# Cross attention scores of the samples: turned keys and TensorE against product-sums on VectorE, with a new order of the sequence buffers

## What is computed

```
xn = rms(h);  p = xn @ w_in
A  = gated DeltaNet (4 heads, chunks of 64; samples: one recurrence step)
B  = latent attention (samples: 2048 cached positions each, in pages)
h += concat(A, B) @ w_out
q  = (rms(h) @ w_xq) as 4 heads of 256
s  = einsum('bthd,bmhd->bhtm', q, mem_k) / 16         # 256 memory tokens
h += einsum('bhtm,bmhd->bthd', softmax(s), mem_v) @ w_xo
h += MoE(rms(h))      # top 4 of 32 experts, w_e1 1024x2048, w_e2 1024x1024 each
y  = rms(h)
```

## Time and profile before

| what | value |
|---|---|
| median of 3 runs | 1478.03 us (1472.29 to 1478.19) |
| the profiled execution: its time | 1474.19 us |
| its span in the trace | 1472.4 us |
| mean granted TensorE clock | 0.977 |
| TensorE busy | 1342.5 us (91%) |
| VectorE busy | 473.3 us (32%) |
| ScalarE busy | 175.9 us (12%) |
| bytes moved | 490.62 MB, mean 333 GB/s |
| `in_w_e` on the chain that ended last | 42% of the span |

### The profile page before, as it was taken

How to read it: one execution, slowest core, us unless ns; L and a number is a source line. 1 busy time by engine, 2 the same in 40 slices (tenths; PEclk the granted TensorE clock), 3 DMA queues, 4 the chain that set the end, 5 groups by cost and what they waited for, 6 DMA issues and landing times.

```text
span 1472.4 us, 19981 instructions
## 1 busy us (share of the span) xinstructions
PE 1342.5 (91%) x8119; PEld 626.1 (43%) x8119; DVE 473.3 (32%) x1082; ACT 175.9 (12%) x343; POOL 48.1 (3%) x45
## 2 busy tenths in 40 slices
PE   8999887999998989999998998998989989889896
PEld 6667543354586453333333233333332333333322
DVE  1856665932033352132222122122221221222213
ACT  1053101221022430000000000000000000000002
POOL 0000211000000420000000000000000000000000
PEclk9999988999999989999999999999999999999999
DMA  9111553636457669999999999999999999999996
GB/s 372 40 36 76 202 209 150 241 112 256 177 223 232 245 254 426 427 426 428 428 428 428 427 428 428 428 428 428 428 428 427 428 428 427 427 427 427 428 427 249
DMA packets 80339, 490.62 MB, mean 333 GB/s; under 512 B 9308, under 2 KB 14528, under 8 KB 28987
## 3 DMA queue, kind: packets, MB, share of 16 engines
q1 hardware_dynamic: 77690, 468.86, 77.2%
q0 software_dynamic: 2304, 20.97, 3.6%
q10 hardware_dynamic: 296, 0.11, 0.0%
HBM read 483.97 MB, written 6.04 MB: 333 GB/s over the span
## 4 chain that ended last, share of the span: by engine, by line
DMA 43%; PE 21%; DVE 2%; ACT 1%; SPq 1%; POOL 1%; issue 1%; DVEq 0%
DMA arena<-in_w_e 42%; PE ps L2032 12%; PE ps L2075 4%; DMA arena<-in_cache_mem_k 1%; PE ps L2103 1%; SPq L1449 1%; PE ps L2117 1%; PE ps L2087 0%; PE ps L2111 0%; POOL arena L2426 0%; POOL arena L2424 0%; DVE arena L2612 0%; DVE arena L2615 0%; DVE arena L2609 0%; PE ps L2062 0%
## 5 line engine op out<-in xcount | busy, mean ns | idle before, releaser
L2032 PE MATMUL ps<-arena 128*64 128x512 f32 x2048 | 460.6, 597 | 54.0 <-DMA arena<-in_w_e 53.0
L2032 PEld LDWEIGHTS ps<-arena 128*64 128x64 f32 x2048 | 146.3, 137 | 346.7 <-issue 293.9
L2075 PE MATMUL ps<-arena 128*64 128x512 f32 x952 | 209.3, 594 | 0.4 <-ACT arena L2289 0.2
L2075 PEld LDWEIGHTS ps<-arena 128*64 128x64 f32 x952 | 67.6, 137 | 136.3 <-issue 128.4
L2609 DVE TENSOR_SCALAR arena<-ps 128x1024 f32<-128x1024 f32 x15 | 18.4, 1225 | 264.7 <-PE ps L2032 264.7
L2627 DVE TENSOR_TENSOR res<-res,ps 128x512 f32<-128x512 f32 x60 | 41.3, 688 | 135.5 <-PE ps L2087 135.5
L2621 DVE COPY arena<-ps 128x512 f32<-128x512 f32 x15 | 10.4, 692 | 209.6 <-PE ps L2075 209.6
L1073 PE MATMUL ps<-arena 32*4 32x512 f32 x640 | 48.9, 657 | 17.5 <-DVE arena L1099 17.5
L1746 PE MATMUL ps<-arena 128*128 128x512 f32 x128 | 55.8, 594 | 0.0
L2018 PE MATMUL ps<-arena 128*128 128x128 bf16 x768 | 54.0, 223 | 1.7 <-DVE arena L2576 1.7
L2087 PE MATMUL ps<-arena 128*128 128x512 f32 x120 | 55.5, 606 | 0.0
(11 more groups left out here) (554 smaller groups left out, 1357.0 us busy)
## 6 DMA issues: line engine op xcount, KB each, us to landing
arena<-in_w_e SPq DMA_DIRECT2D x383, 1024.0 KB, 22.2
arena<-in_w_in SPq DMA_DIRECT2D x8, 1380.0 KB, 17.6
arena<-in_cache_mem_k SPq DMA_DIRECT2D x8, 1024.0 KB, 9.1
arena<-in_w_out SPq DMA_DIRECT2D x2, 2048.0 KB, 8.2
arena<-in_w_xk SPq DMA_DIRECT2D x1, 4096.0 KB, 15.5
arena<-in_w_xv SPq DMA_DIRECT2D x1, 4096.0 KB, 13.6
arena<-in_w_xq SPq DMA_DIRECT2D x1, 4096.0 KB, 23.1
arena<-in_cache_mem_v SPq DMA_DIRECT2D x1, 4096.0 KB, 16.0
```

Source lines behind the costliest of these rows:

```text
L2032: last = pe.matmul(ps[64 * x:64 * x + 64, c, :], xe[:, k, 64 * x:64 * x + 64], weights[x][:, c * 512:(c + 1) * 512], start=False, stop=(k ...
L2075: last = pe.matmul(ps[64 * x:64 * x + 64, 6 + c, :], aT[:, k, 64 * x:64 * x + 64], weights[x][:, j * D + c * 512:j * D + (c + 1) * 512], s ...
```

## The change

Five things are changed.

1. The order of the slots is plain rotation: sequence 6 goes into slot 2 and 7 into slot 3, and GpSimd loads them in the order 4, 5, 6, 7. The half of `w_out` that lies over slot 3 waits for all 8 sequences instead of 7.
2. In the scan's chunk 0, the page step moves behind the state update on VectorE and behind its product on TensorE; the turning of its keys, which was the tail of the last level, moves with it.
3. The mix parts of the prompt's other half for rows 2 and 3 move ahead of the wait for `w_out`'s half 0.
4. `turn_keys`, `KTx` and `qpad` go. 32 small products put the samples' queries into rows of PSUM, ScalarE and VectorE copy them to `q_rows`, two products per sample spread one query row over all 128 partitions in PSUM, and VectorE multiplies raw keys with it and sums (64 `scalar_tensor_tensor` of 128x256 with `accum_out`, one column of `sT` each). 8 products turn `sT` into the bank of the scores. The four `project` of the prompt's `w_xo` part go between the spreads, and VectorE's four joins of the prompt now come ahead of the sample rows', which is the fifth instead of the fourth.
5. ScalarE's order puts the first three bias casts ahead of the exponential. SyncE fills ring slots 1 and 2 ahead of 8 to 11 and 4 to 7, and there are 4 spare buffers instead of 3.

```diff
-    SLOT = (0, 1, 2, 3, 0, 1, 3, 2)
+    SLOT = (0, 1, 2, 3, 0, 1, 2, 3)
...
-        pages_dve(dve, level_step(LEVELS))
+        pages_dve(dve, level_step(LEVELS), False)
...
-        for b in (4, 5, 7, 6):
+        for b in range(NSLOT, DEC):
             pool.wait_ge(sa["pv_done"], max(c for c in range(b) if SLOT[c] == SLOT[b]) + 1)
...
-            for k in chunk_steps(i, 0):
+            for k in chunk_steps(i, 0) if i > 0 else ():
                 pages_dve(dve, k)
...
             last.then_inc(s_ready, 1)
+            if i == 0:
+                turn_keys_of(dve, STEP_SCAN)
+                for k in chunk_steps(i, 0):
+                    pages_dve(dve, k)
...
-            sp.wait_ge(sa["pv_done"], DEC - 1)
+            sp.wait_ge(sa["pv_done"], DEC)
             load_w_out(sp, 0)
...
-            pe.wait_ge(gn["placed"], 1)
+            mix_part(2, range(H, 2 * H))
+            pe.wait_ge(gn["placed"], 2)
+            mix_part(3, range(H, 2 * H))
             pe.wait_ge(wout_gdn_loaded, 16)
...
-    SPARE = 3
+    SPARE = 4
...
+            def spread_query(b):
+                if b >= 2:
+                    pe.wait_ge(sx["scored"], b - 1)
+                for j in range(2):
+                    i = (2 * b + j) % 4
+                    rows = slice(32 * i, 32 * i + DEC)
+                    last = pe.matmul(ps[:, SPREAD_BANKS[b % 2] + j, :], rep1(c_(C_ID, P)[rows, 32 * i + b], [DEC, P]), q_rows[rows, j * 512:(j + 1) * 512],
+                                     start=True, stop=True, tile_position=(32 * i, 0))
+                last.then_inc(sx["spread"], 1)
...
+            for k in range(KD):
+                for i in range(4):
+                    last = pe.matmul(ps[32 * i:32 * i + DEC, 6 + k // 4, (k % 4) * P:(k % 4 + 1) * P], qxT[:, k, SEQ:TOK], ident,
+                                     start=True, stop=True, tile_position=(0, 32 * i))
...
+            def score(b):
+                dve.wait_ge(kx_loaded[b % G], 16 * (b // G + 1))
+                dve.wait_ge(sx["spread"], b + 1)
+                for s in range(2):
+                    if s == 1 and b > 0:
+                        dve.wait_ge(sx["scored"], b)
+                    for h in range(H):
+                        query = ps[:, SPREAD_BANKS[b % 2] + h // 2, (h % 2) * XD:(h % 2 + 1) * XD]
+                        last = nc.vector.scalar_tensor_tensor(products[:, (8 * b + 4 * s + h) % 12], Kx[:, b % G, s, h * XD:(h + 1) * XD], 1.0, query, ALU.mult, ALU.mult,
+                                                              accum_out=sT[:, s, h, b:b + 1])
+                last.then_inc(sx["scored"], 1)
```

More of the change, by code:

```diff
@@ L1303, in scan_pe @@
             last.then_inc(add_made, 1)
+            for k in chunk_steps(i, 0) if i == 0 else ():
+                pages_pe(pe, k)
             for k in chunk_steps(i, 1):
@@ L1465, in build @@
     PARTS = 2 * ((0, 0), (0, 1), (1, 0), (1, 1))
-    cx = {n: sem("cross_" + n) for n in ("keys_stored", "padded", "q_made", "q_moved", "scored", "max", "exp", "probs", "turned", "pt_ready", "out", "out_moved")}
+    cx = {n: sem("cross_" + n) for n in ("keys_stored", "q_made", "q_moved", "scored", "max", "exp", "probs", "turned", "pt_ready", "out", "out_moved")}
     drained = sem("mix_drained")
@@ L1533, in _ @@
             exps(3)
-            act.wait_ge(cx["padded"], 1)
-            for n in range(2 * H):
-                nc.scalar.copy(qpad[:, n].rearrange("p b c -> p (b c)")[:, 0:33 * (DEC - 1) + 1:33], qxT[:, n, SEQ:TOK])
         @block.gpsimd
@@ L1961, in _ @@
             sp.dma_start(pick, const_bf16).then_inc(mo["pick_loaded"], 16)
+            sp.wait_ge(mo["bias_ready"], 1)
+            for n in (1, 2):
+                fill_first(sp, n)
             sp.wait_ge(sx["out"], 1)
@@ L1967, in _ @@
                 fill_first(sp, n)
-            sp.wait_ge(mo["bias_ready"], 1)
-            for n in (1, 2):
-                fill_first(sp, n)
             sp.wait_ge(mo["made"], 5)
-            for i in range(2):
+            for i in range(3):
                 fill(sp, FIRST_SPARE + i, 0, spare[i], spare_full[i])
             sp.wait_ge(mo["logits"], 3)
-            fill(sp, FIRST_SPARE + 2, 0, spare[2], spare_full[2])
+            fill(sp, FIRST_SPARE + 3, 0, spare[3], spare_full[3])
             sp.wait_ge(mo["rounds"], 1)
@@ L2136, in positions @@
                 pe.matmul(ps[0:r, bank, 64:64 + NE], c_(C_BEF, r, r), sel[0:r, t, :], start=not before, stop=True).then_inc(mo["pos"], 1)
-            for m in range(2 * DEC):
-                turn_keys(m)
-                if m >= 2 and m % 2 == 0:
-                    score(m // 2 - 1)
-            score(DEC - 1)
-            pe.wait_ge(wxo_loaded, 16)
-            project(0, 0, 0, range(KD))
+            for k in range(KD):
+                for i in range(4):
+                    last = pe.matmul(ps[32 * i:32 * i + DEC, 6 + k // 4, (k % 4) * P:(k % 4 + 1) * P], qxT[:, k, SEQ:TOK], ident,
+                                     start=True, stop=True, tile_position=(0, 32 * i))
+            last.then_inc(sx["q_turned"], 1)
+            pe.wait_ge(wxo_loaded, 16)
+            project(0, 0, 0, range(0, 3))
+            pe.wait_ge(sx["q_act"], 1)
+            pe.wait_ge(sx["q_dve"], 1)
+            spread_query(0)
+            spread_query(1)
+            project(0, 0, 0, range(3, 6))
+            spread_query(2)
+            project(0, 0, 0, range(6, KD))
+            project(0, 1, 1, range(0, 1))
+            spread_query(3)
+            project(0, 1, 1, range(1, 4))
+            spread_query(4)
+            project(0, 1, 1, range(4, KD))
+            spread_query(5)
+            pe.wait_ge(mo["joined"], 1)
+            project(1, 0, 0, range(0, 4))
+            spread_query(6)
+            project(1, 0, 0, range(4, 7))
+            spread_query(7)
+            project(1, 0, 0, range(7, KD))
+            pe.wait_ge(mo["joined"], 2)
+            project(1, 1, 1, range(0, 4))
+            pe.wait_ge(sx["scored"], DEC)
+            for s in range(2):
+                for h in range(H):
+                    last = pe.matmul(ps[32 * h:32 * h + 32, 4, s * P:(s + 1) * P], sT[:, s, h, :], ident, start=True, stop=True, tile_position=(0, 32 * h))
+            last.then_inc(sx["s_turned"], 1)
+            project(1, 1, 1, range(4, KD))
             pe.wait_ge(sx["probs"], 1)
@@ L2189, in _ @@
             positions(0, 1, ())
-            project(1, 1, 5, range(3, 5))
             turn(1, 0, 2)
@@ L2304, in cast_part @@
                 return nc.scalar.copy(x_part(t, i)[:, a:b], left[t][:, a:b])
-            for m in range(2 * DEC):
-                act.wait_ge(sx["turned"], m + 1)
-                n = m // 2
-                if n >= 2:
-                    act.wait_ge(sx["scored"], n - 1)
-                nc.scalar.copy(KTx[:, n % 2, 0:4, (m % 2) * P:(m % 2 + 1) * P], ps[:, 2 * (m % 2), :].rearrange("p (k n) -> p k n", k=4)).then_inc(sx["moved_act"], 1)
-            act.wait_ge(sx["max"], 1)
-            nc.scalar.activation(pS[:, :], ps[:, 4, 0:MEM], ACT.Exp, bias=small[:, 46:47], scale=X_SCALE, accum_out=small[:, 47:48]).then_inc(sx["exp"], 1)
+            act.wait_ge(sx["q_turned"], 1)
+            for i in range(4):
+                rows = slice(32 * i, 32 * i + DEC)
+                last = nc.scalar.copy(q_rows[rows, 0:512], ps[rows, 6, :])
+            last.then_inc(sx["q_act"], 1)
             act.wait_ge(mo["cleared"], 1)
-            act_chain.link(act, nc.scalar.activation(stat[:, 12:13], stat[:, 4:5], ACT.Sqrt))
             act.wait_ge(mo["b_loaded"], 6 * 16)
```

104 lines of the change are left out of this document (44 added, 60 removed).

## The result

The changed kernel takes 1466.83 us (median of 18 runs), the kernel before 1476.22 (18 runs beside them). The ratio is 0.9942, interval 0.9927 to 0.9958: 8.6 us shorter (6.2 to 10.8; the medians lie 9.4 apart). I had said 1458, a gain of 17.5 us. The direction was right and the time lies in the range, but **the gain is half of what I forecast**. The profiled execution of the changed kernel took 1471.10 us, with a span of 1469.1; it is among the longest six of the 18 runs, which go from 1462.20 us at a mean granted clock of 0.978 to 1473.55 at 0.972, with 0.968 the lowest clock. TensorE is busy for 1334.2 us (1342.5 before), VectorE for 492.1 (473.3), ScalarE for 168.1 (175.9).

A forecast was written before the change was run, and what follows sets the result against it. The stream of expert weights, not arithmetic, was taken to bound the kernel. Terms 10.6 + 4.5 + 2.45 = 17.5 us gave 1456.7 from the profiled execution, 1460.5 from the median; forecast 1458 us, range 1446 to 1469.

The forecast's parts named there:

- The frame: Expert weight stream sets the pace; the end moves only with first hidden step, fills out before it, and 2.453 us per fill.
- rival 2: Scan: the rotation fails, sequence 6 or 7 still stalls, up to all 8.3 us stay; 1461 to 1466 us, chance 0.12.
- Part S: Expert weight fills: a fourth spare buffer puts one fill more out before the first slot comes free, 2.45 us.
- Part B: Scan: rotation of the buffers ends VectorE's wait for sequence 6; 8.3 + 1.7 + 0.6 = 10.6 us.
- The 0.6 of chunk 0: Scan's chunk 0: state update now ahead of one turning of 1.2 us, between 0 and 1.2 on the path, 0.6 taken.
- my 1.7 for that block: Scan, TensorE: slow score block L1073 behind the wait, 3.62 us against 1.92, goes with the stall; 1.7 us.
- the clock as a risk: Between 530 and 540 the low 1.2 GHz stretch may start earlier; sets part E's end bound, 3 to 8 us.
- Part E: Sample cross scores: product-sums on VectorE and reordered ScalarE bring the first hidden step to 539.0, 4.5 us earlier.
- my first rival: Sample cross part: bias rows land early, by 478.7, everything there 3 to 4 us sooner; about 1453 us, chance 0.13.
- my fourth rival: Sample cross scores: product-sums from 0.89 us eat the whole gain; at 1.05, about 1485 us, slower; chance 0.04.
- my third rival: Sample cross scores: VectorE product-sums at half rate, 0.82 us each, 13.4 of 17.5 us gone; about 1470 us, chance 0.11.

The follow-up runs named there:

- chunk0_before: The changed kernel with chunk 0's page step back ahead of the state update, rotation kept: 1464.87 us, ratio 0.9941.
- scores_only: The changed kernel with the scan's part undone, leaving the new cross scores, ScalarE order and fourth spare: 1473.88 us, ratio 0.998.
- before_again: The unchanged kernel before, profiled once more: 1480.58 us, one execution.
- rotation_only: The kernel before with only the scan's part (slot rotation, load order, chunk 0, wait for `w_out`, mix parts): 1467.97 us, ratio 0.9937.
- bias_early: The changed kernel with the six loads of the biases ahead of the second half of the keys: 1455.15 us, ratio 0.9864.
- exp_first: The changed kernel with ScalarE's exponential behind the first bias cast instead of the third: 1468.14 us, ratio 0.9946.
- pool_later: The changed kernel with GpSimd's second subtraction held back until the probabilities are normalised: 1462.16 us, ratio 0.9898.
- busy_wait: The changed kernel with eight products into a free bank in TensorE's wait for the probabilities: 1465.12 us, ratio 0.9931.

## Where the prediction held and where it failed

**The frame held.** The end follows the first hidden step, 928.9 to 930.8 us later in 13 profiles. The sum failed in each of its three terms: of 10.6 + 4.5 + 2.45 us the profiles show about 6.3, 3 and none, and the 3 come with the old cross part as well. That the time lies in the range is no merit of the mechanism. It comes near rival 2 (1461 to 1466), but the stall that this rival kept is gone.

**Part S failed: 2.45 us forecast, none seen.** The step was "one fill more is out before the first slot comes free: 368 instead of 369". The count is right; that the end comes a fill sooner for it is not. With a fill less to do, the stream idled between 600 and 640, as I read it until TensorE gave slots back. I had taken it for granted that a fill saved at the start is a fill saved at the end, and not asked where the stream would first catch up with TensorE.

**Part B failed by its size: 10.6 forecast, about 6.3 seen** (mean stretch from the first piece to the cross part 257.1 in three old scans, 250.8 in ten new ones). The rotation itself is as worked out: from the third update to the fourth it is 251.78 - 238.61 = 13.2 us where it was 257.67 - 234.62 = 23.05, 9.9 less: the wait of 8.3 and a slow score block went. The 0.6 of chunk 0 did not (chunk0_before). But my 1.7 for that block was no gain of the rotation, since another one stands a chunk earlier. TensorE's timeline of the changed kernel:

```profile
225.93 3.62 PE L1073 MATMUL ps<-arena 32*4 32x512 f32 x32 [1.89 <-DVE arena L1099]
```

This block took 1.93 us before (at 223.63) and in scores_only, 3.61 in before_again, and 2.6 to 3.6 in all ten profiles with the new scan; the granted clock from 225 to 230 is 0.66 in the changed kernel and was 1.00 before. The whole scan is 57.8 us instead of 66.0 in the mean, 8.2 less. The other 1.9 were lost between scan and cross part (191.1 to 193.0), which I had let shift as a block; the two long low stretches at the mix parts make half of that (252.5 and 256.1 against 249.9, the mean of the other eight). I had priced the clock as a risk in part E alone.

**Part E failed: 4.5 forecast, 3 seen beside the old scan (scores_only) and nothing beside the new one**, by steps that were wrong in both directions. First, its base: the 543.47 - 449.0 = 94.5 us that I reckoned from held keys turned at 0.86 of the clock; with the new scan the old code needs 91.3 (rotation_only), so about 3 of the 4.5 belonged to the clock (one profile of that kernel). The product-sum took 0.342, not 0.48, and the last bias row landed at 477.1, not 482.4, so the exponential was 5 us early (28.2 + 14.4 = 42.6 us behind the cross part's start, 47.8 forecast). That was the condition of my first rival, but its 1453 did not come. The normalisation then took 5.39 us: I gave that step no price, as it was 0.35 before, and did not ask what GpSimd would be doing at its new time, though the row for exactly this stood in my fourth rival (L2463's 1.65 us end 0.05 us behind GpSimd's instruction, at 511.26 + 2.12). The output products behind it ran at half clock for a part, 8.79 us instead of 7.07. Less these two losses, 5.04 and 1.72, the rest of my chain was well sized: 19.3 us from the exponential to the sample rows' join (L2565 ends at 517.61; forecast 19.9) and 22.2 from there to the first hidden step (forecast 22.3). Over all runs the new cross part also goes with a lower mean granted clock, 0.968 to 0.978 in the 18 runs of the changed kernel, 0.978 to 0.982 in the ten of rotation_only; in which stretch, runs without a profile don't show. What I said of the late bias rows, that they hold the exponential, was right, and it was the larger lever: bias_early takes 11 us of it.

The Trainium skill ("SBUF — State Buffer", section "SBUF: two separate sides") says that VectorE and GpSimd share one pair of ports as an exclusive lock, held for a whole instruction, which VectorE needs in its two-port fast modes, or with two inputs in SBUF against a GpSimd operation that reads SBUF. The runs agree: 5.39 us ended by GpSimd's end, 0.35 when GpSimd was held back or done, and 417 ns for product-sums with one operand in PSUM in the midst of both subtractions. So that rule would have named the step that I missed. The half rate of my third rival is not seen, nor the price of the fourth.

The Trainium skill ("TensorE: Matmul & The Clock Gate", section "Part 1: The HAM clock gate (the "warmup" mystery)") says that the default state is throttled and that activity releases it. The rows here agree in part: half clock behind a wait, as in exp_first from 495 to 500, and 1.00 in the experts' windows. But from 285 to 295 of the changed kernel TensorE was busy for the whole 10 us at 0.50 and 0.57. When the clock falls in a given execution no run here could tell ahead.

## What to carry to other kernels

Where a change moves an instruction in time, look up what the other engines do at its new time, not only who waits for it: a VectorE operation from SBUF to SBUF that lands beside a long GpSimd operation can take until that ends (the normalisation did; the reciprocal of 128x1 ahead of it did not). A late small load ahead of other work on an in-order engine (here three times 384 KB of biases between megabytes of keys) can hold the whole chain behind it; order loads by when the chain needs them. And a gain of 8 us is hardly more than the scatter of the clock between two profiles of one kernel, which was 5 us here before the scan began: take stretches between marks, over several profiles.

## What the runs showed that I had not expected

- One VectorE instruction of 128x256 takes 0.35 or 5.39 us, depending on GpSimd alone (exp_first, pool_later, changed).
- Accumulating product-sums on VectorE come every 0.342 us: the accumulator's read of 82 ns is hidden.
- A spread of two products on two row groups takes 1.13 us for four instructions of 512 columns; L1705 with four of the same width on one group takes 1.98.
- Keeping TensorE busy through a wait (busy_wait) kept its clock there and changed the time by nothing that can be measured; the low clock came later instead.
